# GpSimd makes the parameters and the powers of lambda of the S5 stage early, during the latent attention stage

## The reference, cut to what matters

```python
def s5_mixer(h, w_in, lam_re, lam_im, log_step, b_re, b_im, c_re, c_im, d_skip, w_glu, b_glu, w_out):
    u, z = jnp.split(h @ w_in, 2, axis=-1)
    lam = lax.complex(lam_re, lam_im)
    step = jnp.exp(log_step)[:, None]
    lam_bar = jnp.exp(lam * step)
    b_bar = ((lam_bar - 1.0) / lam)[..., None] * lax.complex(b_re, b_im)
    bu = jnp.einsum('gpi,btgi->btgp', b_bar, ug)                 # ug: u in 128 groups of 16
    _, states = lax.associative_scan(_diag_linear_combine, (a_seq, bu), axis=1)
    y = jnp.einsum('gip,btgp->btgi', c, states).real.reshape(...) + d_skip * u
    y = jax.nn.gelu(y)
    y = y * jax.nn.sigmoid(y @ w_glu + b_glu) * jax.nn.silu(z)
    return y @ w_out
```

## Time and profile before

| what | us |
|---|---|
| median of 3 runs | 3825.73 |
| the profiled execution, its own time | 3821.77 |
| its span in the trace | 3820.1 |
| PE busy | 3466.4 (91%) |
| DVE busy | 2466.8 (65%) |
| ACT busy | 1562.2 (41%) |
| POOL busy | 142.1 (4%) |

### The profile page before, as it was taken

One profiled execution on the slowest core, in us unless ns is written; L12 is line 12 of the kernel. 1 busy time (PEld: TensorE's weight loads), 2 busy tenths in 40 slices (PEclk: granted clock), 3 DMA queues, 4 the chain that ended last, 5 costly groups with the idle time before them and its releaser, 6 DMA issues.

```text
span 3820.1 us, 48701 instructions
## 1 busy us (share of the span) xinstructions
PE 3466.4 (91%) x18186; PEld 2959.2 (77%) x18186; DVE 2466.8 (65%) x3189; ACT 1562.2 (41%) x1853; POOL 142.1 (4%) x176
## 2 busy tenths in 40 slices
PE   5899999979999988888699999878998799999998
PEld 5777787767888767776589988678887678888886
DVE  4677777776555564554699976846555665665655
ACT  3344444434444333332267654333333344334342
POOL 0000000000000000000122200100000000000000
PEclk8899999989999998998799999999999999999999
DMA  5455555534444443333232245566665355455553
GB/s 207 150 192 187 195 189 190 195 142 182 178 177 170 160 160 121 123 131 109 90 111 100 100 144 201 184 213 219 220 231 198 123 193 190 177 198 185 182 187 126
DMA packets 89265, 642.83 MB, mean 168 GB/s; under 512 B 10177, under 2 KB 10257, under 8 KB 11713
## 3 DMA queue, kind: packets, MB, share of 16 engines
q1 hardware_dynamic: 83376, 607.16, 44.0%
q0 software_dynamic: 5776, 34.13, 2.8%
HBM read 638.02 MB, written 3.23 MB: 168 GB/s over the span
## 4 chain that ended last, share of the span: by engine, by line
PE 60%; DVE 18%; issue 7%; DVEq 6%; DMA 4%; ACT 4%; POOL 0%; ACTq 0%; SPq 0%; POOLq 0%
PE banks L682 16%; PE banks L683 16%; PE banks L684 16%; DVE WL L666 6%; DMA raw<-in_stream 4%; ACT WH L658 3%; DVE xc L1254 1%; PE banks L1399 1%; DVEq L2415 1%; PE banks L699 1%; DVEq L2405 1%; PE banks L700 1%; PE banks L980 1%; PE banks L701 1%; PE banks L730 1%
## 5 line engine op out<-in xcount | busy, mean ns | idle before, releaser
L666 DVE TENSOR_TENSOR WL<-raw,WH 128x2048 fp32r<-128x2048 f32 (+2 forms) x575 | 1248.8, 2174 | 702.2 <-ACT WH L658 693.7
L658 ACT ACTIVATE WH<-raw 128x2048 fp32r<-128x2048 f32 (+2 forms) x575 | 1045.6, 1821 | 1083.3 <-DMA raw<-in_stream 504.7
L682 PE MATMUL banks<-WH,XH 128*128 128x512 f32 (+2 forms) x2784 | 1069.8, 384 | 73.0 <-DVE WL L666 32.0
L684 PE MATMUL banks<-WH,XL 128*128 128x512 f32 (+2 forms) x2784 | 1045.1, 375 | 0.0
L683 PE MATMUL banks<-WL,XH 128*128 128x512 f32 (+2 forms) x2784 | 1044.9, 375 | 0.0
L682 PEld LDWEIGHTS banks<-WH,XH 128*128 128x128 f32 x2784 | 535.9, 192 | 171.6 <-issue 60.3
L684 PEld LDWEIGHTS banks<-WH,XL 128*128 128x128 f32 x2784 | 535.2, 192 | 82.0
L683 PEld LDWEIGHTS banks<-WL,XH 128*128 128x128 f32 x2784 | 536.1, 193 | 77.5 <-issue 0.5
L682 PE MATMUL banks<-WH,YH 128*128 128x512 f32 x976 | 395.0, 405 | 13.7 <-DVE acc L771 8.4
L683 PE MATMUL banks<-WL,YH 128*128 128x512 f32 x976 | 389.5, 399 | 0.0
L684 PE MATMUL banks<-WH,YL 128*128 128x512 f32 x976 | 387.2, 397 | 0.0
(11 more groups left out here) (405 smaller groups left out, 3541.8 us busy)
## 6 DMA issues: line engine op xcount, KB each, us to landing
raw<-in_stream SPq DMA_DIRECT2D x575, 1024.0 KB, 4.8
gain<-in_gains POOLq DMA_DIRECT2D x9, 1024.0 KB, 5.1
arow<-acs_scratch POOLq DMA_DIRECT2D x8, 1024.0 KB, 4.9
offs<-in_ln_b POOLq DMA_DIRECT2D x4, 1024.0 KB, 7.4
acc<-in_x SPq DMA_DIRECT2D x2, 1024.0 KB, 6.7
src<-in_mem POOLq DMA_DIRECT2D x1, 2048.0 KB, 9.0
toep<-rvec_scratch POOLq DMA_DIRECT2D x4, 512.0 KB, 8.4
out_y<-src SPq DMA_DIRECT2D x2, 1024.0 KB, 3.9
```

The lines of the kernel that those rows point to most:

```text
L658: nc.scalar.activation(WH[:, n.first % PARTS, at], raw[:, n.first % RAWS, at], ACT.Copy).then_inc(hi_ready, 1)
L666: nc.vector.tensor_tensor(WL[:, n.first % PARTS, at], raw[:, n.first % RAWS, at], WH[:, n.first % PARTS, at].bitcast(F32), ALU.subtract).t ...
L682: nc.tensor.matmul(out, xh[:, k0 + k, at], wh[:, k, lo:hi], start=start, stop=False)
L684: ins = nc.tensor.matmul(out, xl[:, k0 + k, at], wh[:, k, lo:hi], start=False, stop=stop)
```

## The change

- The transfer of S5's parameters (`par5`) is issued in the MLA stage, to a buffer of its own place (`small`), as are the temporaries `tmp5`. `pows5` and `dt5`, `turns5`, `jump5` trade places between two regions of memory.
- The exponential of the step size stands on ACT right behind the rotary sines; the exponential of the radius and two sines stand behind the first pass over the heads.
- `|lambda|^2` and its reciprocal stand on DVE in the head part of MLA, behind its eighth split.
- All other parameters and the powers are computed by POOL in a new function `s5_powers`, behind its power for the latents. Where DVE had `scalar_tensor_tensor`, POOL has two instructions.
- POOL's transfers of `d5` and `bg5` and three memsets stand ahead of the layer norm, behind a wait for the last head.
- On DVE the S5 stage begins with the split of slot n+4 and the first tables; the scaling of the residual follows the output table, and the two small preparations (`bg5`, `jump5`) the split of n+6.

```diff
@@ mla_scalar
         nc.scalar.activation(cossin[:, 0, :, :], ang[:, :, :], ACT.Sin, scale=0.5).then_inc(act_done, 1)
+        act.wait_ge(par_loaded, 16)
+        nc.scalar.activation(tmp5[:, TMP, :], par5[:, LSTEP, :], ACT.Exp).then_inc(step_ready, 1)
...
         body(At(MLA_HEAD), At(MLA_SLOT + 9), At(0), True)
+        act.wait_ge(theta_ready, 1)
+        nc.scalar.activation(tmp5[:, RADIUS, :], tmp5[:, RADIUS, :], ACT.Exp)
+        nc.scalar.activation(tmp5[:, SIN1, :], tmp5[:, THETA, :], ACT.Sin)
+        nc.scalar.activation(tmp5[:, SINH, :], tmp5[:, THETA, :], ACT.Sin, scale=0.5).then_inc(sines_ready, 1)
@@ mla_vector
         for s in range(8):
             split_low(dve, At(MLA_SLOT + s + LEAD))
+        dve.wait_ge(par_loaded, 16)
+        nc.vector.tensor_tensor(tmp5[:, CRE, :], par5[:, LRE, :], par5[:, LRE, :], ALU.mult)
+        nc.vector.tensor_tensor(tmp5[:, CIM, :], par5[:, LIM, :], par5[:, LIM, :], ALU.mult)
+        dve.drain()
+        nc.vector.tensor_tensor(tmp5[:, CRE, :], tmp5[:, CRE, :], tmp5[:, CIM, :], ALU.add)
+        dve.drain()
+        nc.vector.reciprocal(tmp5[:, TMP2, :], tmp5[:, CRE, :]).then_inc(norm5_ready, 1)
         dve.wait_ge(slots_used, MLA_SLOT + 9)
@@ s5_scalar
-        reply()
-        nc.scalar.activation(tmp5[:, TMP, :], par5[:, LSTEP, :], ACT.Exp).then_inc(act_done, 1)
-        reply()
...
-        nc.scalar.activation(tmp5[:, SINH, :], tmp5[:, THETA, :], ACT.Sin, scale=0.5).then_inc(act_done, 1)
@@ s5_vector
-        dve.wait_ge(xt_done, 32)
-        scale_residual(dve)
-        dve.wait_ge(act_done, ask("act"))
...
         split_low(dve, At(n + 4))
-        dve.wait_ge(act_done, ask("act"))
...
+        dve.wait_ge(s5_loaded, 64)
+        dve.wait_ge(zeroed, 2)
+        dve.wait_ge(powers_ready, 1)
...
         input_tables(0)
         split_low(dve, At(n + 5))
         output_tables(0)
+        dve.wait_ge(xt_done, 32)
+        scale_residual(dve)
         split_low(dve, At(n + 6))
@@ s5_powers, new
+        pool.wait_ge(par_loaded, 16)
+        pool.wait_ge(step_ready, 1)
+        pool.wait_ge(norm5_ready, 1)
...
+        pool.drain().then_inc(theta_ready, 1)
+        nc.gpsimd.tensor_scalar(co5[:, TURN4, :], theta, 4 / TWO_PI, None, ALU.mult)
+        pool.wait_ge(sines_ready, 1)
...
+        for k in range(1, 5):
+            nc.gpsimd.tensor_tensor(t1, re[:, k - 1, :, :], lr, ALU.mult)
+            nc.gpsimd.tensor_tensor(t2, im[:, k - 1, :, :], li, ALU.mult)
+            nc.gpsimd.tensor_tensor(t3, im[:, k - 1, :, :], lr, ALU.mult)
+            nc.gpsimd.tensor_tensor(t4, re[:, k - 1, :, :], li, ALU.mult)
+            pool.drain()
+            nc.gpsimd.tensor_tensor(re[:, k, :, :], t1, t2, ALU.add)
+            nc.gpsimd.tensor_tensor(im[:, k, :, :], t3, t4, ALU.subtract)
+            pool.drain()
@@ POOL's main list
         power(pool, served_pool[0], 0, 4)
+        s5_powers(pool)
+        pool.wait_ge(headl_ready, MIX_HEAD)
+        pool.dma_start(d5[:, :], a["s5_d"]).then_inc(s5_loaded, 16)
+        pool.dma_start(bg5[:, :], a["s5_bglu"]).then_inc(s5_loaded, 16)
...
+        pool.drain().then_inc(zeroed, 1)
         norm_powers(pool)
```

More of the change, by code:

```diff
@@ L346, in program @@
     with ExitStack() as s:
-        pows5 = sb("pows5", [P, 2, 5, 2, 64], within=s)
         x5 = sb("x5", [P, 2, 4, 64], within=s)
         ring5 = sb("ring5", [P, 4, 64], within=s)
+        dt5 = sb("dt5", [P, 4, P], within=s)
+        turns5 = sb("turns5", [P, 2, T], within=s)
+        jump5 = sb("jump5", [P, P], within=s)
     with ExitStack() as s:
@@ L2243, in s5_scalar @@
         act.wait_ge(slots_used, n + 4)
[L2244 removed]
+        act.wait_ge(zeroed, 2)
         stack(0, (0, 1), range(16))
@@ L2330, in s5_vector @@
         n = S5_SLOT
-        par, tmp = par5, tmp5
-        dve.wait_ge(par_loaded, 16)
-        dve.drain().then_inc(act_asked, 1)
-        dve.wait_ge(xt_done, 32)
-        scale_residual(dve)
-        dve.wait_ge(act_done, ask("act"))
-        nc.vector.tensor_tensor(tmp[:, RADIUS, :], par[:, LRE, :], tmp[:, TMP, :], ALU.mult)
-        nc.vector.tensor_tensor(tmp[:, THETA, :], par[:, LIM, :], tmp[:, TMP, :], ALU.mult)
-        dve.drain()
-        whole_turns(dve, tmp[:, THETA, :], tmp[:, CRE, :])
@@ L2341, in s5_vector @@
-        dve.drain().then_inc(act_asked, 1)
-        dve.wait_ge(zeroed, 1)
-        nc.vector.tensor_scalar(co5[:, TURN4, :], tmp[:, THETA, :], 4 / TWO_PI, None, ALU.mult)
-        for q in range(4):
-            at = slice(32 * q, 32 * q + 32)
-            nc.vector.tensor_copy(jump5[at, 32 * (3 - q):32 * (3 - q) + 32], ident[at, 32 * q:32 * q + 32])
-        split_low(dve, At(n + 4))
-        dve.wait_ge(act_done, ask("act"))
-        nc.vector.tensor_tensor(tmp[:, SINH, :], tmp[:, SINH, :], tmp[:, SINH, :], ALU.mult)
@@ L2365, in s5_vector @@
-        nc.vector.tensor_tensor(tmp[:, RADIUS, :], tmp[:, SINH, :], par[:, LIM, :], ALU.mult)
-        dve.drain()
-        nc.vector.reciprocal(tmp[:, TMP, :], tmp[:, TMP, :])
-        nc.vector.tensor_tensor(tmp[:, CRE, :], tmp[:, CRE, :], tmp[:, TMP2, :], ALU.add)
-        nc.vector.tensor_tensor(tmp[:, CIM, :], tmp[:, RADIUS, :], tmp[:, CIM, :], ALU.subtract)
-        nc.vector.tensor_scalar(tmp[:, SINH, :], tmp[:, SINH, :], 1.0, None, ALU.add)
-        dve.drain()
-        re, im = pows5[:, 0, :, :, :], pows5[:, 1, :, :, :]
@@ L2389, in s5_vector @@
-        nc.vector.tensor_scalar(bg5[:, :], bg5[:, :], 0.5, None, ALU.mult)
+        split_low(dve, At(n + 4))
+        dve.wait_ge(s5_loaded, 64)
+        dve.wait_ge(zeroed, 2)
+        dve.wait_ge(powers_ready, 1)
         flat = q4.rearrange("p a t -> p (a t)")
@@ L2476, in s5_vector @@
         output_tables(0)
+        dve.wait_ge(xt_done, 32)
+        scale_residual(dve)
         split_low(dve, At(n + 6))
+        nc.vector.tensor_scalar(bg5[:, :], bg5[:, :], 0.5, None, ALU.mult)
+        for q in range(4):
+            at = slice(32 * q, 32 * q + 32)
+            nc.vector.tensor_copy(jump5[at, 32 * (3 - q):32 * (3 - q) + 32], ident[at, 32 * q:32 * q + 32])
+        dve.drain()
         for c in range(CHUNKS5):
```

115 lines of the change are left out of this document (63 added, 52 removed).

## The result

| | runs | median us | lowest to highest |
|---|---|---|---|
| kernel before | 4 | 3823.83 | 3819.51 to 3827.88 |
| changed kernel | 4 | 3802.57 | 3801.70 to 3805.26 |

The ratio is 0.9948, with a 95% interval from 0.9934 to 0.9963. Six more runs of the changed kernel in a second comparison (experiment e2) gave 3808.88 with a ratio of 0.9958 [0.9946, 0.9971]. Its ten runs lie between 3801.6 and 3814.1, with a mean of 3805.8. Each group set against the kernel before of its own comparison, by means, is 20.7 and 15.6 us shorter, 17.7 over the ten. The profiled execution took 3805.26 us, its span 3803.3, which is 16.8 less than before.

A forecast was written before the change was run, and what follows sets the result against it. The prediction took the first scan's start, held by DVE's work ahead of its first input table, as the bound; -17.0 + 1.5 + 1.1 + 1.0 = -13.4, so 3825.73 - 13.4 = 3812.3 us, range 3806 to 3821.

The forecast's parts named there:

- S5 start, -17.0: Start of the S5 stage: the first scan starts at 1903.1 instead of 1920.07, -17.0 us.
- the upper bound of 5.4: S5 start, transfer of slot n+6: 4.8 us taken; 5.4 of waiting, also seen, would make the gain -16.4.
- ACT behind the rotary sines +1.5: MLA head: a table load of 1.28 and an exponential of 0.2 delay ACT's next split, +1.5 us.
- DVE's four instructions +1.1: MLA head, behind DVE's eighth split: two products, a sum and a reciprocal delay what is queued, +1.1 us, between 0 and 1.3.
- Rival 1: MLA head: the moved work is hidden in waits for transfers, costs 0, leaving -17.0 and 3808.7 us; chance 12%.
- POOL beside DVE +1.0: MLA heads: POOL's products slow DVE instructions beside them, few on the path, +1.0 us, bounds 0 and 19.8.
- a pass that grows by over 1 us and low halves that grow beside POOL: MLA heads: signs that the forecast is wrong; it expected passes over the heads of nearly the same length.
- The table loads in the loop, 0: MLA passes over the heads: ACT's 3.3 us behind the first pass is covered by a 5.47 us wait, cost 0.
- rival 2: MLA loop: table loads there and the pair ahead are on the path, +5.9, so -7.5 and 3818.2 us; chance 16%.
- Rival 3: MLA heads: each of 43 POOL products holds up DVE by 0.46, +19.8, so +5.4 and 3831.1 us; chance 8%.
- The drain of a table load: ACT's table switches: about 1380 ns of drain each would cost 2.8 us more, some -10.6 in all; left out.
- Nothing for what follows the S5 stage: Stages behind S5: the sum had no term for them and ended at -13.4 us.

The follow-up runs named there:

- e5: The changed kernel with POOL's powers 1 to 4 filled by memsets in place of products and sums; 3806.05 us, ratio 0.9961.
- e9: The kernel before with 80 unused one-column memsets on POOL behind the latents' power; one profiled execution, bias-table stretch 65.4 us.
- e10: The changed kernel with 64 unused one-column memsets at the top of DVE's list; one profiled execution, bias-table stretch 69.6 us.
- e4: The changed kernel with the bias table filled by eight long-row transfers from the weight stream, so with other biases; 3800.65 us, ratio 0.9940.
- e7: e6 with a shorter S5 start: first sines ahead of split n+6, jump5 earlier, scalings behind the chunk loop, PE's first inputs earlier; 3805.27 us, ratio 0.9962.
- e11: The changed kernel with POOL's transfers of d5 and bg5 back at their earlier place in its queue; one profiled execution, bias-table stretch 66.1 us.
- e12: The same kernel as e7, timed once more; 3803.28 us, ratio 0.9952.
- e3: The kernel before with the bias table filled by eight long-row transfers from the weight stream, so with other biases; 3817.68 us, ratio 0.9984.
- e8: The kernel before with only the residual's scaling on DVE moved behind the first output table; 3818.36 us, ratio 0.9991.
- e6: The changed kernel with the work ACT and DVE took over in MLA put into their waits, no table load left in the loop; 3803.84 us, ratio 0.9957.

## Why the forecast was wrong in its total, step by step

- **S5 start, -17.0:** right in mechanism, order of events and size (-16.7 at the first scan, -16.5 over the stage). The wait for the transfer was 5.43, the upper bound of 5.4, and `jump5` doubled beside POOL; those are the 0.3.
- **ACT behind the rotary sines +1.5, DVE's four instructions +1.1:** right where they stand (1.46 and 1.20, the latents' power 2.8 late). What is left of them depends on PE's clock behind them: 0.7 by 1513 in the changed kernel, the whole of it up to 1749 in e5, 0.2 at e5's end. Rival 1 had them hidden in waits of the head, and they were not.
- **POOL beside DVE +1.0:** the mis-sized term within MLA. It is 2.8, all of it in the first pass over the heads (e5 has none there). The contention is 1.1 of it at PE's wait; the larger part is the clock of PE, at half its speed behind the longer wait. The prediction named a pass that grows by over 1 us and low halves that grow beside POOL as signs of being wrong, and both came. That MLA's sum fits all the same, 3.2 measured for 3.6 forecast, is luck: 1.8 too little for POOL against 2.1 of the head's that came back.
- **The table loads in the loop, 0:** right; the lag behind the kernel before is 3.4 at 1531 and at 1801, with the loads in each pass between, and rival 2 is out. Rival 3 would have needed 19.8; POOL's products were met at few places.
- **The drain of a table load,** which the Trainium skill's page "ScalarE: Activation LUTs" puts at about 1380 ns (section "What ACT_TABLE_LOAD costs"): not seen. The exponential starts 1.29 after the load began.
- **Nothing for what follows the S5 stage:** this is the step that failed. The sum ends with S5, and gives no reason why the stages behind it should keep their length. A difference of -3.3 in the bias-table stretch (-3.5 and -3.1) and -0.2 to -0.4 ahead of it belongs to the change as it stands. e9 and e10 tip that stretch by adding idle instructions to one list, so the change, which lengthens POOL's list and shortens DVE's, can have tipped it in the same way. With it the stages sum to -16.9, the profiled execution has -16.8, and the ten runs say -17.7. ("In the loop nothing is changed" is about the loop over chunks, and held.)
- **The rest of the -21.3** is spread: four runs of the changed kernel that all came out low. In the next six the difference was 15.6. The failed step alone would not have left the stated range: 3825.73 less the ten runs' 17.7 is 3808.0, inside it. What took the median to 3802.57 are these four low runs; the kernel before, too, came out 1.9 lower here (3823.83) than the 3825.73 from which the forecast counts.

The variable stretch 2683 to 2957 shows itself in the granted clock too. Windows of 40 us at the same place of it in the changed kernel and in e2:

```profile
2867.00:2907.00 40.00, 37.31 (x220) 36.01 (x219) 20.27 (x27) 15.42 (x23) 0.00 (x0) 1.00 0.63 230
```

```profile
2866.00:2906.00 40.00, 37.18 (x213) 36.29 (x212) 19.46 (x26) 14.01 (x20) 0.00 (x0) 0.96 0.63 221
```

A clock of 0.96 instead of 1.00 goes with 7 matmuls fewer and a loss of 1.2 us at the next head. Kernels with the change (e2, e4, e7, e10, e11, e12) and without it (e3, e8) had such losses, of 2.4 to 5.7 us in all; what starts them was not tried.

## What to carry to other kernels

Sum the touched stages from the trace, but take a difference below about 0.1% for what the untouched stages can do by themselves: 80 idle instructions more in one list, or 64 in another, tipped a crowded transfer stretch far behind them by 4.0 and 3.6 us. When work is moved to POOL, ask for each place not how long POOL works but what DVE has to deliver there in time: the same products cost 2.8 us beside DVE's low half and rotation ahead of a waiting PE, and nothing 40 us earlier. A microsecond more of waiting on PE can cost as much again and more behind it, in the clock. And follow a delay from place to place before calling it paid or free: e5's end shows 0.2 where 3.3 stood for most of the stage.

## What was not expected of the hardware

- A small POOL product beside a DVE low half waits for nearly the whole of it: POOL's product took 2.51 instead of 0.46 (e6), DVE's low half 2.57 instead of 2.29. The losses are one-sided: 2.05 for POOL, 0.28 for DVE. The Trainium skill (page "SBUF — State Buffer", section "Who interferes with whom") has them lock each other out for a whole instruction, and these rows agree. From it I had concluded only that a short POOL instruction costs DVE little. That is so; what it costs PE is another matter.
- POOL's first tensor_scalar behind tensor_tensor came after a gap of 2.4 us (1425.96 to 1428.35) that the profile puts down to issue (2.39); it came once in e2, e5 and e6 too, in the same place, and not again afterwards.
- Instructions whose result is not used, in idle time, changed the length of a stretch by 4.0 us (e9) and 3.6 us (e10), 1000 us later and more.
